# Mixture-of-experts weight streaming on one core: another assignment of the nine SBUF slots, two refills in halves, a later second gather half

## What is computed

```python
def moe(h, w_r, b_r, w_gu, b_gu, w_dn, b_dn):
    logits = (t @ w_r + b_r).astype(jnp.float32)
    top_v, top_i = lax.top_k(logits, TOP_K)          # 4 of 32 experts for each row
    ...
    def body(e, acc):
        gu = t @ w_gu[e] + b_gu[e]                    # 1024 -> 2048
        g, u = jnp.split(gu, 2, axis=-1)
        g = jnp.minimum(g, SWIGLU_LIMIT)
        u = jnp.clip(u, -SWIGLU_LIMIT, SWIGLU_LIMIT)
        hdn = (u + 1.0) * (g * jax.nn.sigmoid(SWIGLU_ALPHA * g))
        y = hdn @ w_dn[e] + b_dn[e]                   # 1024 -> 1024
        return acc + comb[:, e][:, None] * y
    out = lax.fori_loop(0, N_EXPERTS, body, jnp.zeros_like(t))
```

## Time and profile before

| | |
|---|---|
| runs shown | 1288.73, 1289.26, 1289.80 us |
| median | 1289.26 us |
| profiled execution | 1291.79 us |
| its span | 1290.0 us |
| TensorE busy / DMA engines busy over the span | 94% / 88% |
| expert loop, from its first gather to the end | 362.2 to 1290.0 us |

### The profile page before, as it was taken

How to read it: one execution, slowest core, us unless ns; L and a number is a source line. 1 busy time by engine, 2 the same in 40 slices (tenths; PEclk the granted TensorE clock), 3 DMA queues, 4 the chain that set the end, 5 groups by cost and what they waited for, 6 DMA issues and landing times.

```text
span 1290.0 us, 13991 instructions
## 1 busy us (share of the span) xinstructions
PE 1213.5 (94%) x5550; PEld 577.2 (45%) x5550; DVE 410.2 (32%) x774; ACT 174.0 (13%) x311; POOL 33.1 (3%) x50
## 2 busy tenths in 40 slices
PE   6999999999999999999999998999899999989897
PEld 1777478888544343333333332433333333334332
DVE  5178896884422221120222102111301211021203
ACT  3222004230221010010101001000101010010000
POOL 3300200001000000000000000000000000000000
PEclk9999999999999999999999999999999999999999
DMA  9943442779489999999999999999999999999996
GB/s 373 383 174 108 148 156 107 301 286 401 179 354 426 401 428 428 428 429 428 428 430 429 427 428 429 428 428 430 429 428 428 429 428 428 430 429 427 427 426 247
DMA packets 50707, 475.73 MB, mean 369 GB/s; under 512 B 3970, under 2 KB 4130, under 8 KB 24051
## 3 DMA queue, kind: packets, MB, share of 16 engines
q1 hardware_dynamic: 49426, 471.26, 87.8%
q0 software_dynamic: 1248, 4.03, 0.9%
HBM read 474.22 MB, written 1.05 MB: 368 GB/s over the span
## 4 chain that ended last, share of the span: by engine, by line
PE 66%; DMA 28%; DVE 2%; ACT 1%; issue 1%; SPq 0%; DVEq 0%
DMA ring_sb<-w_down 26%; PE bank L1149 20%; PE bank L1249 11%; PE bank L859 10%; PE bank L1104 5%; PE bank L1265 4%; PE bank L1020 3%; PE bank L868 3%; PE bank L1049 2%; DMA area_sb<-w_down 2%; PE bank L1118 1%; DVE area_sb L1867 1%; PE bank L784 1%; PE bank L798 1%; PE bank L1010 1%
## 5 line engine op out<-in xcount | busy, mean ns | idle before, releaser
L1149 PE MATMUL bank<-ring_sb,area_sb 128*64 128x512 f32 x1536 | 400.2, 598 | 16.4 <-DMA ring_sb<-w_gu 16.4
L1149 PEld LDWEIGHTS bank<-ring_sb,area_sb 128*64 128x64 f32 x1536 | 124.4, 137 | 226.1 <-issue 213.7
L1249 PE MATMUL bank<-ring_sb,area_sb 128*64 128x512 f32 x608 | 165.9, 598 | 18.7 <-DMA ring_sb<-w_down 16.8
L1149 PE MATMUL bank<-area_sb 128*64 128x512 f32 x512 | 171.2, 594 | 0.0
L859 PE MATMUL bank<-area_3h_sb,ring_sb 128*128 128x256 f32 x704 | 154.2, 379 | 0.0
L859 PEld LDWEIGHTS bank<-area_3h_sb,ring_sb 128*128 128x128 f32 x704 | 133.2, 190 | 20.1 <-issue 1.8
L2123 DVE TENSOR_SCALAR area_sb<-bank 128x512 f32<-128x512 f32 x32 | 22.1, 692 | 304.2 <-PE bank L1149 304.2
L2147 DVE TENSOR_TENSOR area_sb<-area_sb,bank 128x512 f32<-128x512 f32 x64 | 44.0, 688 | 211.9 <-PE bank L1265 211.9
L2154 DVE TENSOR_TENSOR area_sb<-bank,area_sb 128x512 f32<-128x512 f32 x32 | 22.1, 692 | 230.4 <-PE bank L1249 218.0
L1249 PEld LDWEIGHTS bank<-ring_sb,area_sb 128*64 128x64 f32 x608 | 51.2, 137 | 89.7 <-issue 89.7
L1509 ACT ACTIVATE area_sb<-bank 128x512 f32<-128x512 f32 (+1 forms) x80 | 44.0, 551 | 333.5 <-PE bank L1104 255.6
(11 more groups left out here) (278 smaller groups left out, 807.8 us busy)
## 6 DMA issues: line engine op xcount, KB each, us to landing
ring_sb<-w_gu SPq DMA_DIRECT2D x96, 2048.0 KB, 26.2
ring_sb<-w_down SPq DMA_DIRECT2D x38, 2048.0 KB, 25.8
area_sb<-w_gu SPq DMA_DIRECT2D x32, 2048.0 KB, 30.3
area_sb<-w_down SPq DMA_DIRECT2D x16, 2048.0 KB, 20.4
ring_sb<-w_in SPq DMA_DIRECT2D x14, 2048.0 KB, 10.1
ring_sb<-w_ada SPq DMA_DIRECT2D x12, 2048.0 KB, 10.3
area_3h_sb<-w_down SPq DMA_DIRECT2D x8, 2048.0 KB, 35.6
ring_sb<-w_branch SPq DMA_DIRECT2D x3, 2048.0 KB, 9.5
```

The costliest lines, as they stand in the source:

```text
L1149: ins = pe.matmul(bank[n][r, :], xT[:, k, r], w[e][:, n * 512:(n + 1) * 512], start=False, stop=k == KT - 1, skip_group_check=True)
L1249: ins = pe.matmul(bank[4 + n][r, :], hidT[:, k, e * SLOTS:(e + 1) * SLOTS], w[e][:, kk, n * 512:(n + 1) * 512], start=False, stop=k == KT ...
```

## The change

`SLOT_OF` is another table, and a new list `AHEAD` names the nine chunks that are issued ahead of a body: 0 to 7 and 14. Chunk 8 now goes into slot 0, 9 into slot 1, 10 to 13 into slots 2 to 5, chunk 14 into slot 8 and 15 into slot 6; pair b's 16 to 21 into slots 0 to 5, 22 into slot 7, 23 into slot 8. The order of issue is 0 to 7, 14, 8, 9, 10, 11, 12, 13, 15, 16 ... 23. Chunks 8 and 9 are issued as halves of 1 MB (`load_split`): the first halves of both when block k = 0 of pair a has been used (a new semaphore, `first_rows_used`), the second halves when block k = 1 has. TensorE waits for two more semaphores ahead of the first half of `down` in pair a. In pair a the second gather half moves behind block k = 1, and `gate_bias` for pair a moves from the end of the body before (or from `router`) behind the first gather half.

```diff
-SLOT_OF = list(range(MOE_SLOTS)) + list(range(7)) + list(range(8))
+SLOT_OF = [0, 1, 2, 3, 4, 5, 6, 7] + [0, 1, 2, 3, 4, 5, 8, 6] + [0, 1, 2, 3, 4, 5, 7, 8]
+AHEAD = [0, 1, 2, 3, 4, 5, 6, 7, 14]
...
             n = PAIR_CHUNKS * b + c
+            if n in (8, 9):
+                eng.wait_ge(early_landed[n - 8], i * 16 + 16)
...
+            def load_split(i, j):
+
+                for part in range(2):
+                    for n in (8, 9):
+                        e = n % 2
+                        row = 0
+                        src = a["w_down"][0, bass.ds(j * 4 + e, 1), row:row + 4 * P, :]\
+                            .rearrange("e (p k) m -> p (e k) m", k=4)[:, 2 * part:2 * part + 2, :]
+                        dst = moe_slot(0, n)[:, 2 * part * D:2 * (part + 1) * D].rearrange("p (k m) -> p k m", k=2)
+                        if part == 0:
+                            sp.wait_ge(first_rows_used, i + 1)
+                            sp.dma_start(dst, src).then_inc(early_landed[n - 8], 16)
+                        else:
+                            wait_slot(i, n)
+                            sp.dma_start(dst, src).then_inc(moe_chunk_landed(0, n), 16)
...
             def body(i, j, last):
-                for n in range(MOE_SLOTS, BODY_CHUNKS):
-                    load(i, j, n, last)
+                load_split(i, j)
+                for n in range(10, BODY_CHUNKS):
+                    if n not in AHEAD:
+                        load(i, j, n, last)
                 if not last:
-                    for n in range(MOE_SLOTS):
+                    for n in AHEAD:
                         load(i + 1, j + 1, n)
...
                 pe.wait_ge(bias_landed, 16 * 6)
-                gate_bias(0, 0, 0)
                 rank(0)
...
-                for g in range(2):
+                for g in range(1 + b):
                     gather(i, s, b, g)
+                if b == 0:
+                    gate_bias(i, p, 0)
...
+                        elif b == 0 and k == 0 and n == 3 and e == 1:
+                            ins.then_inc(first_rows_used, 1)
...
                 for k in range(KT):
+                    if b == 0 and k == 2:
+                        gather(i, s, b, 1)
...
                     if b == 0:
                         gate_bias(i, p, 1)
-                    elif not last:
-                        gate_bias(i + 1, p, 0)
```

More of the change, by code:

```diff
@@ L446, in build_layer @@
         weights_used = sem("weights_used")
+        first_rows_used = sem("first_rows_used")
+        early_landed = [sem(f"early_landed{i}") for i in range(2)]
         gate_up_done = sem("gate_up_done")
@@ L653, in one_pass @@
                         wait_freed(NF + n - 2 - WEIGHT_SLOTS)
-                    elif n == 8:
+                    elif n == 14:
                         sp.wait_ge(products_ready, JOB["logits1"] + 1)
@@ L1276, in body, with one_pass @@
                         gate_bias(i, p, 1)
-                    elif not last:
-                        gate_bias(i + 1, p, 0)
                 for n in range(4):
                     scatter(i, "b", 1, n)
-            def one_pass(p, first=False):
-                if not first:
-                    gate_bias(p * BODIES, p, 0)
+            def one_pass(p):
                 with pe.Fori(0, BODIES - 1) as j:
@@ L1289, in _ @@
             router()
-            one_pass(0, first=True)
+            one_pass(0)
             pe.wait_ge(flag_ready, 1)
```

## The result

| | before | after |
|---|---|---|
| median of 15 runs of each | 1290.91 us | 1294.53 us |
| ratio of the runs | | 1.0027, 95% interval 1.0019 to 1.0034 |
| span of the profiled execution | 1290.0 us | 1292.4 us |
| granted TensorE clock, mean | 0.995 | 0.982 |

The change makes the kernel 0.27% slower, some 3.6 us. The forecast was 0.3 us slower with an upper end of 1292.2; the measured median lies above it, and against its own kernel before (1290.91, not the 1289.26 of the first three runs) the move is 3.6 us where I had up to 2.9.

What follows compares the result with a forecast made beforehand. Loads were taken to set the pace from 452 us on, TensorE the end. Chunk 11's +4.90, pauses −3.5 and halves +0.8, less 1.92 of waiting, gave +0.3 us: span 1290.3, median 1289.5 us, range 1286.8 to 1292.2.

Steps and rivals of the forecast that it cites:

- What bounds the kernel, and that the end is TensorE's in the last body: Loads set the pace from 452 us on; after the change TensorE's 47.2 us behind chunk 11 outlast the loads' 44.1 us.
- Net cost 4.90 − 1.92 = +2.98 us: Last body: chunk 11 lands 4.90 us later in the order, less TensorE's 1.92 us of waiting for loads behind it.
- the wait of 1.04 us: Ahead of down in another body: split into 0.69 us for ScalarE's copy and 0.35 us for the load.
- The term is 0 by the rows, and up to +1.7: Half-clock stretches behind long waits are hidden by the next wait; up to +1.7 us if exposed in the last body.
- The 13.6 us: Half-clock cost by the skill's rule alone, without cover: eight stretches at +1.7 us each.
- The pauses: Idle DMA time at 372 to 376 and 424 to 428 us falls from 5.3 to 1.8 us: −3.5 us.
- The halves: Rows of 8 KB instead of 16 load slower, 0.1 us a body in eight bodies: +0.8 us, bounds 0 and 1.1.
- (b): Rival: the pauses only move, so the saving shrinks; at no saving +3.8 us, 1293.1 us; chance 0.12.

Runs made afterwards that it cites:

- the best kernel: The change with halves and chunk 14 ahead of 8 in the first body only, natural order and whole chunks elsewhere: 1289.02 us, 0.9985 to the kernel before.
- The pair of runs with one load moved: Halves in the first body only, chunk 14 ahead of 8 in first and last body against first body only: 1293.15 us against 1289.02 us.
- the partner: The change with halves and chunk 14 ahead in the first body only, run beside the version with chunk 14 ahead in the last body too: 1289.02 us.
- The filled version: The change plus idle TensorE matmuls in two waits of the last body, 8 ahead of down in pair a and 2 in pair b: 1292.81 us, 1.0016.

## Why the prediction was wrong

The loss of the change, put together from the profiles: chunk 11 of the last body is 3.3 us later; of the 1.92 us that TensorE waited behind it before, ScalarE's copy needed 1.30 anyway, so 0.6 was slack; the clock took 1.5. That is 3.3 − 0.6 + 1.5 = 4.2 of the 4.5 us of loop time. The forecast had 2.2 − 1.92 + 0 = 0.3.

Two rows of ScalarE in the trace before, to set beside the earlier trace rows:

```profile
1263.99 0.63 ACT L1518 ACTIVATE area_sb<-area_sb 128x512 f32<-128x512 f32 x1 [2.17 <-DVE area_sb L2123]
1264.53 0.85 ACT L1509 ACTIVATE area_sb<-bank 128x256 f32<-128x256 f32 x2
```

- *What bounds the kernel, and that the end is TensorE's in the last body*: right. The loads run at 428 GB/s through all middle bodies, the long wait stands ahead of down in pair a only, and TensorE doesn't wait for chunks 20 and 21 any more. Both land 1.6 us earlier than before, counted from the issue of chunk 6, and chunk 11 lands at 1218.16, 0.1 us ahead of TensorE's start on it. That the late chunk 11 is what is paid is shown by moving that one load, in one body, out of the change and into the best kernel (0.9985 there against 1.0018).
- *"Net cost 4.90 − 1.92 = +2.98 us"*: **this step failed**, and with it the clock's term of the next point. The 1.92 us were read as slack against the loads. A second wait lay under them. By the two rows above, TensorE's transposes end at 1263.51 + 0.72 = 1264.23, a sigmoid (L1518) holds ScalarE until 1264.6, and the copy of the turned rows is done at 1265.38. In the change the same copy is ready 1.30 us after TensorE asks for it, more than the 0.69 us of the other bodies. I had split the wait of 1.04 us in just this way and didn't do it here. So the slack was 0.6 us, and the cost by this reading 4.90 − 0.6 = 4.3 us. The pair of runs with one load moved measured +4.1; that the two agree so well is partly luck, since the partner had spent its slack on the clock.
- *"The term is 0 by the rows, and up to +1.7"* for the clock: the middle bodies went as forecast. Each from the third on has its stretch at half clock at the long wait, the wait for chunks 10 and 11 takes it up (0.40 us or less is left of it), and taking all of these stretches away changed nothing that shows. In the last body's pair b such a stretch was exposed, for 1.5 us, the largest single error of the sum. I had the amount as a bound, for just a stretch behind the landing of chunk 11 in the last body, and put it into the sum at 0. The Trainium skill's rule, TensorE: Matmul & The Clock Gate, HAM oscillation, that a TensorE which waits for data again and again drops to half clock each time, agrees with the six waits of 4.8 to 6.1 us of the change, each of which has a fall; of the waits of up to 2.3 us in the kernel before, most have none. The 13.6 us that I had worked out for it without cover did not come.
- *The pauses, "−3.5 us"*: 2.7 were saved. The bytes are late by 0.6 us at chunk 10, which was issued 379.76 − 360.08 = 19.7 us after the start of the loop and not 19.1: block k = 0 starts 3.33 us after the first gather instead of 3.07, and the sequence of small steps adds up. The places of the pauses were right.
- *The halves, +0.8*: 1.2 by the rate, just over the bound of 1.1. With the pauses this gives −2.7 + 1.2 = −1.5 us for the loads, where the forecast had −2.7.
- *The rivals*: (b) had the right side and the right size at its end, "at no saving +3.8 us", but its mechanism isn't what happened: over half of the idle time was saved. I had given it 0.12. That its +3.8 is close to the measured +3.6 is luck. The place of the loss was in the forecast itself, with too small a price. Four terms, the slack, the clock, the pauses and the halves, were each off by 0.4 to 1.5 us in the same direction; with the clock's bound of 1.7 us on top of rival (b)'s +3.8 the range would have reached 1294.8.

What stays open: in the profile before, the clock doesn't fall at down of pair b of the last body, though it does in eight of the ten profiles of kernels without filled waits (1.4 to 2.8 us; the other one without is the second profile of the kernel with halves and chunk 14 ahead in the first body only). The unprofiled runs of the kernel before suggest that it often falls there or at another place where it costs: of the 98 that stand beside the experiments, the 22 with a granted clock of 0.995 or more took 1289.9 us in the mean, the 17 with 0.992 or less 1293.1. They don't say where it falls. If it is there, then less of the 3.6 us belongs to the clock; the rest of the sum, 3.3 − 0.6 = 2.7 us, is the larger part either way. The filled version puts the clock's share in the change at about 1.4 us.

## What to carry to other kernels

A wait seen in a trace hides every shorter wait at the same place: before counting it as slack, look for the second to last thing that the instruction needs. When loads set the pace, an order of loads that helps the pipeline to fill may be wrong for its end; peel the first body and use the special order there alone (here 0.15% faster than before instead of 0.27% slower). And in this load-bound loop a longer wait in the middle bodies, half clock included, cost nothing that showed; only in the last body was it paid.

## What the runs showed of the hardware

With a wait of 4.8 to 6.1 us the clock fell in the wait and stayed low for 2.9 to 5.1 us of the work behind it (down's first 16 matmuls take 5.12 to 6.18 us in the six bodies instead of 3.65, and half of a stretch at half clock is lost). Stretches in the last body of the change:

```profile
1204.00:1206.00 2.00, 0.00 (x0) 0.00 (x0) 0.00 (x0) 0.00 (x0) 0.00 (x0) 0.75 1.03 430
1206.00:1208.00 2.00, 0.00 (x0) 0.00 (x0) 0.00 (x0) 0.00 (x0) 0.00 (x0) 0.50 1.05 442
1208.00:1210.00 2.00, 1.39 (x4) 0.58 (x6) 0.00 (x0) 0.00 (x0) 0.00 (x0) 0.50 0.98 418
1210.00:1212.00 2.00, 2.00 (x8) 0.57 (x6) 0.00 (x0) 0.00 (x0) 0.00 (x0) 0.54 1.08 459
1212.00:1214.00 2.00, 2.00 (x11) 0.64 (x8) 0.00 (x0) 0.00 (x0) 0.00 (x0) 1.00 0.95 393
```

The price was 1.6 us here (5.24 us for 16 matmuls instead of 3.65), and 2.3 us in the third body (5.90 us), though the wait was shorter there, 4.77 us. A short wait can bring it as well: at the end of the change TensorE waits 0.32 and 1.30 us with four transposes (in the profile's count) between, and its next 16 matmuls fall on

```profile
1266.00:1268.00 2.00, 1.26 (x4) 0.60 (x6) 1.88 (x4) 0.59 (x2) 0.00 (x0) 0.61 1.04 414
1268.00:1270.00 2.00, 2.00 (x6) 0.54 (x4) 0.94 (x4) 0.00 (x0) 0.00 (x0) 0.53 1.00 395
```

With two or three idle matmuls in that wait they ran at full clock, in the profiles of all three kernels that had such filling; without it, in two of ten.
